# The weight load of the next FFN unit goes ahead of the LN1 row store on SyncE's queue

## The reference

```python
merged = gates[:, :, 0] * y_conv + gates[:, :, 1] * y_attn + gates[:, :, 2] * y_mem
x = layer_norm(DEEPNORM_ALPHA * x + merged @ w_o, ln1_g, ln1_b)
gate, up = jnp.split(x @ w_ffn_in, 2, axis=-1)          # w_ffn_in: 1024 x 5632
ffn = (jax.nn.silu(gate) * up) @ w_ffn_out              # w_ffn_out: 2816 x 1024
return layer_norm(DEEPNORM_ALPHA * x + ffn, ln2_g, ln2_b)
```

## Time and profile before

| What | Value |
|---|---|
| median of three runs | 977.96 us |
| profiled execution, device time | 978.9 us |
| its span (slowest core, core 7) | 977.9 us |
| spans of the eight cores | 970.8 to 977.9 us |
| TensorE matmul busy | 941.3 us (96%) |
| VectorE busy | 613.6 us (63%) |
| ScalarE, GpSimd busy | 438.9 and 291.7 us |

### The profile page before, as it was taken

The page is one execution under the profiler, slowest core; times in us unless marked ns, Lnnn a source line. Parts: engine busy times, 40 slices in busy tenths (PEclk is TensorE's granted clock), DMA queues, the critical chain, the costliest instruction groups (busy, mean ns, idle before and its releaser), DMA issues.

```text
span 977.9 us, 16532 instructions; the slowest of 8 cores (970.8 to 977.9 us)
## 1 busy us (share of the span) xinstructions
PE 941.3 (96%) x5556; PEld 441.9 (45%) x5556; DVE 613.6 (63%) x997; ACT 438.9 (45%) x709; POOL 291.7 (30%) x296
## 2 busy tenths in 40 slices
PE   3999999999999999999999999999999999999997
PEld 1454544554444444444445444444444444444444
DVE  0323476667766857566668798876476666663555
ACT  1125657576663354444544455554122444443212
POOL 3200000112135334334321344444433233334331
PEclk9999999999999999999999999999999999999999
DMA  8898023374258999512486365665433323220232
GB/s 131 153 178 165 24 77 101 64 149 72 45 86 121 117 150 132 76 65 57 95 252 266 87 166 148 161 147 126 158 129 129 108 86 109 86 87 1 86 108 87
DMA packets 39683, 112.12 MB, mean 115 GB/s; under 512 B 4976, under 2 KB 16888, under 8 KB 38608
## 3 DMA queue, kind: packets, MB, share of 16 engines
q0 software_dynamic: 11104, 41.16, 29.0%
q1 hardware_dynamic: 28496, 69.91, 22.3%
HBM read 132.49 MB, written 30.47 MB: 167 GB/s over the span
## 4 chain that ended last, share of the span: by engine, by line
PE 83%; DMA 6%; DVE 5%; issue 3%; ACT 3%; SPq 0%; DVEq 0%; POOL 0%; ACTq 0%; POOLq 0%
PE ps L233 81%; DMA esink<-sinkp 2%; DMA arena<-w_q 2%; DMA arena<-w_bf_cache 1%; DMA gexp_scratch<-arena 1%; ACT arena L597 1%; ACT arena L645 1%; PE ps L1270 1%; DVE arena L1318 1%; DVE arena L1206 1%; DVE arena L1202 0%; DVE arena L807 0%; SPq L147 0%; DVE arena L806 0%; DVE arena L590 0%
## 5 line engine op out<-in xcount | busy, mean ns | idle before, releaser
L233 PE MATMUL ps<-arena 128*128 128x512 bf16 (+5 forms) x5146 | 925.7, 357 | 28.3 <-DMA arena<-xt 16.3
L233 PEld LDWEIGHTS ps<-arena 128*128 128x128 bf16 (+1 forms) x5146 | 421.9, 98 | 515.1 <-issue 69.0
L1315 ACT COPY arena<-ps 128x512 f32<-128x512 f32 x132 | 76.6, 586 | 137.3 <-PE ps L233 137.2
L1325 POOL TENSOR_TENSOR arena<-arena 128x512 bf16<-128x512 f32 x66 | 89.2, 1351 | 151.9 <-DVE arena L1318 143.8
L1318 DVE TENSOR_TENSOR arena<-arena,ps 128x512 f32<-128x512 f32 x132 | 88.0, 684 | 40.3 <-PE ps L233 39.4
L940 POOL TENSOR_TENSOR arena<-arena 128x512 f32<-128x512 f32 (+1 forms) x48 | 63.9, 1339 | 104.2 <-DVE arena L931 104.2
L1184 ACT ACTIVATE arena<-arena 128x1024 bf16<-128x1024 f32 x31 | 32.7, 1056 | 80.7 <-DVE arena L1474 69.8
L931 DVE SCALAR_TENSOR_TENSOR arena<-arena,ps 128x512 f32<-128x512 f32 x72 | 49.2, 684 | 23.9 <-ACT arena L927 18.0
L147 POOL DMA_DIRECT2D arena<-w_g x21 | 11.3, 545 | 168.4 <-PE ps L233 167.2
L923 DVE TENSOR_TENSOR arena<-arena,ps 128x512 f32<-128x512 f32 x54 | 37.1, 686 | 35.2 <-ACT arena L920 19.7
L1206 DVE SCALAR_TENSOR_TENSOR arena<-arena,rs 128x1024 bf16<-128x1024 f32 (+2 forms) x33 | 56.5, 1716 | 1.6
(11 more groups left out here) (117 smaller groups left out, 552.3 us busy)
## 6 DMA issues: line engine op xcount, KB each, us to landing
arena<-w_bf_cache SPq DMA_DIRECT2D x44, 512.0 KB, 3.9
arena<-u_scratch SPq DMA_DIRECT2D x64, 135.0 KB, 3.2
arena<-x SPq DMA_DIRECT2D x16, 512.0 KB, 13.9
y_scratch<-arena SPq DMA_DIRECT2D x16, 512.0 KB, 4.3
arena<-y_scratch SPq DMA_DIRECT2D x16, 512.0 KB, 3.6
out<-arena SPq DMA_DIRECT2D x15, 512.0 KB, 2.6
arena<-w_f POOLq DMA_DIRECT2D x22, 256.0 KB, 5.0
arena<-w_g POOLq DMA_DIRECT2D x9, 512.0 KB, 18.5
```

Source lines behind the costliest of these rows:

```text
L233: return pe.run(lambda: nc.tensor.matmul(out, lhsT, rhs, start=start, stop=stop, skip_group_check=onto), deps, inc)
L1315: return act.run(lambda: nc.scalar.copy(buf, ps[:, b, :]), deps)
L1325: return pool.run(lambda: nc.gpsimd.tensor_tensor(out=dst, in0=up, in1=gate, op=ALU.mult), deps)
```

## The change

The store list is no longer emptied inside `d_lines` and `d_rows`. A new function `y_stores` empties it. `d_chain` calls it first, as before in effect. In the first pass the head of each unit now calls `load_w1(u + 2)` and then `y_stores()`; the call of `load_w1` inside `f1_period` then finds the load already issued and does nothing.

```diff
-    def d_lines(t, lo, hi):
+    def y_stores():
         while y_pend:
             y_pend.pop(0)()
+
+    def d_lines(t, lo, hi):
         if lo <= t - 4 < hi:
             d_Tpe(t - 4)
...
     def d_rows(t, lo, hi):
-        while y_pend:
-            y_pend.pop(0)()
         if lo <= t - 2 < hi:
             d_C(t - 2)
...
     def d_chain(t, lo, hi):
+        y_stores()
         d_lines(t, lo, hi)
         d_rows(t, lo, hi)
...
     for u in range(22):
         t = 10 + u // 2
+        load_w1(u + 2)
+        y_stores()
         f1_period(u, u - 1 if u else None, extra=(lambda: d_rows(t, 8, 16)) if u % 2 else lambda: None)
```

## The result

The changed kernel takes 975.97 us (median of 21 runs), the kernel before 977.54 us (21 runs): ratio 0.9982, 95% interval 0.9976 to 0.9989. By the ratio that is 1.8 us less (1.1 to 2.3), by the medians 1.6; faster, but within the 0.5% that I had called no change. Forecast: 976.3 us. Some executions of every kernel here have the cores of one die at a lower granted clock and are longer; ratios leave these out, and where a whole group of runs has it, I give the mean of the slowest core of the other die with twice its standard error.

The account below looks back on a forecast made before the run. TensorE bounds the kernel; its stage can give back 2.78 us on core 7. Core 7: 977.9 - 1.96 - 0.56 = 975.4, with 1.0 us around the span 976.4; forecast 976.3 us, range 974.6 to 979.0.

Parts of the forecast that it names:

- What the load waited for: SyncE's queue: the even load waited only behind the store for `d_Y`; freed, it goes from 581.56 to about 579.4.
- Time to landing: Even unit's weight load, issue to landing: 5.1 us taken, landing at 584.5; with 8.2 us, at 587.6.
- The cost of a wait: First FFN pass: VectorE's fold may be 1.29 us late before TensorE stalls; 1.96 and 0.56 us come back on core 7.
- Rival 2: VectorE becomes the bound: 0.26 us stalls in all seven even units, 1.8 us against 2.5 gained; 978.2 us, chance 0.10.
- the 0.89 us: VectorE's on-time fold: second instruction 1.31 us instead of 0.42, so it ends 2.37 us earlier, not 3.26; sum unchanged.
- The stall of 0.26 us: TensorE on core 7, before 572.29: no fold wait precedes it, so counted as staying; at most 0.26 us goes too.
- The sum: Core spans after removing stalls: core 7 975.4, core 3 975.0, core 0 974.5, core 4 975.4; slowest 975.4 us.
- Rival 1: Nothing shows in the time: stalls are chance meetings of transfers and another core takes over; 977.9 us, chance 0.20.
- Rival 3: Late store delays the odd unit's load and fold, if that load takes 11.9 us; 983.4 or 990.1 us, chance 0.05.

Follow-up runs that it names:

- the dose run: The changed kernel, but each even unit's weight load also waits for the fold ending the odd unit before, some 3.9 us later; ratio to the kernel before 1.010.

## Why the prediction was right

- **What the load waited for.** Right. Freed of the store, it goes out at 579.29, where I had worked out 579.4 for a core with almost the same times.
- **Time to landing.** I took 5.1 us; 5.5 was measured, and the store behind it took 5.2 instead of the 3.3 of the earlier trace rows; the two now overlap. Over the 56 even loads of the eight cores the median is 4.5 us (3.1 to 7.5), before it was 5.1 (4.2 to 8.2): the load gains a little by its place as well as by its time.
- **The cost of a wait, wait less 1.29 us.** Right for the even folds between the first and the last: 47 of 48 pairs of the dose run are at 1.28 to 1.30. It needs TensorE at a granted clock of 1.00, and it doesn't cover the small stalls of 0.41 and 0.33 us behind the first and the last even fold, which come after shorter waits.
- **Rival 2, VectorE as the bound.** It fell. The second fold instruction does take 1.31 us in every even unit now, beside GpSimd's multiply (586.64 to 588.17 us on core 0), but the 0.89 us are inside VectorE's slack. The lock described in the Trainium skill (SBUF — State Buffer, SBUF: two separate sides) leads one to expect this, and the trace agrees.
- **The stall of 0.26 us.** Wrong. I counted it as staying, because no fold wait was listed before it; it went too. In the earlier trace rows one sees only the load at 581; the one before it had landed at 561.61, just as VectorE came free, and the chain of waits did start at that load. A wait too short to be listed was still first in the chain. The other cores of the same trace show it too: six have a stall of 0.41 or 0.42 us between 568 and 572 us, each some 10 us behind a listed fold wait of 0.25 to 1.55 us, and core 2 has neither. After the change none of the eight cores has such a stall.
- **The sum.** The span of the profiled core was to fall to 975.4; the slowest is at 974.9, and the device time 975.97 against 976.3. Against the median it is 1.6 to 1.8 us where I had 1.7. The sum took one stall each for cores 3, 0 and 4, but their trace has 2.62, 1.95 and 0.84 us of them; it came out close because core 7 set it. That the median runs gain about what I said rests on a guess (that their worst core met smaller stalls) which no trace shows, so there the closeness is in part luck.
- **Rival 1, another core takes over.** Half true, and core 7 was slow "for another reason too", as this rival has it. TensorE's first wait, for its first input, lasted 13.76 us there and 10.91 on core 5; core 7 was 4.3 us behind core 5 before the stage and 7.1 behind it, so the stage made 2.8 of the 7.1. In the profiled run of the changed kernel the slowest core is one with a spell of lower clock at 200 to 250 us; over the 20 runs the slowest core differs from run to run, and in 10 of them it is at a mean clock of 0.996. That this is why the median gains 1.8 us and not the 2.5 of the profiled core is likely and not shown.
- **Rival 3.** The mechanism is real but needed three times the store. Its margin was mis-sized, though. I had 5.5 us that hide the odd load and 1.29 more, a stall from 11.9 us to landing on. The 5.5 were read behind the largest stall, where VectorE was late itself. In the changed kernel the odd load lands at 590.2 and its fold is due at 593.87, so 3.7 us hide it, and there is no 1.29 behind it: a load of 8.0 us is just in time, and one of 11.1 us stalled TensorE by 3.23.
- **Both causes together.** The prediction did not ask which of the two ahead of the load, wait or transfer, was at fault. Neither alone made a stall in the traces.

## What to carry to other kernels

On an in-order DMA queue, put the transfer whose data is due soonest first, and behind it the one that waits for a compute engine: here seven swaps of two DMAs, with nothing added, gave back all of TensorE's listed stalls of the stage. Before costing such a stall, pair each wait with the idle time it causes; if the difference is constant it is the slack, and it says at once which dose is free and which isn't. Take the pairs from every core and from the first and last periods too, and look at the granted clock beside them. The gain of such a change is bounded by the idle time in its stage on the slowest core, and the next slowest core takes over soon after.

## What the runs showed that I had not expected

An extra 512 KB in front of a load costs 13 us over seven loads (some 10.5 with the clock taken off) and behind it nothing, though the 16 DMA engines were only 0.71 busy in the stage of the run that paid. An odd load queued behind three 512 KB stores took 12.4 us once; in the changed kernel it takes 4.5. And 2.6 us of compute (the three fold instructions), put behind the next period's two `plus` in VectorE's order, cost 14 us, more than all late loads of the stage together.
